# A two-block transformer step in one kernel: the first mixer's query rows made once, their turned halves moved by transfers

## The reference, cut to what matters

```python
c_q, c_kv, k_rope = split(h @ w_in)            # 384, 256 and 32 columns
q  = (rmsnorm(c_q, q_norm) @ w_uq).reshape(B, S, 16, 64 + 32)
kv = (rmsnorm(c_kv, kv_norm) @ w_ukv).reshape(B, S, 16, 64 + 64)
q_rope = apply_rotary(q[..., 64:], cos, sin)   # x1*cos - x2*sin, x1*sin + x2*cos
k_rope = apply_rotary(k_rope, cos, sin)        # one for all 16 heads
s = (q_nope @ k_nope^T + q_rope @ k_rope^T) * scale
o = softmax(causal(s)) @ v
```

## Time and profile before

| | us |
|---|---|
| median of 3 runs | 1406.35 |
| lowest, highest | 1406.14, 1406.98 |
| the profiled execution | 1407.12 |
| its span in the profile | 1405.3 |
| TensorE busy | 1392.9 |
| VectorE, ScalarE, GpSimd busy | 915.3, 740.8, 73.9 |

### The profile page before, as it was taken

One profiled execution on the slowest core, in us unless ns is written; L12 is line 12 of the kernel. 1 busy time (PEld: TensorE's weight loads), 2 busy tenths in 40 slices (PEclk: granted clock), 3 DMA queues, 4 the chain that ended last, 5 costly groups with the idle time before them and its releaser, 6 DMA issues.

```text
span 1405.3 us, 21648 instructions
## 1 busy us (share of the span) xinstructions
PE 1392.9 (99%) x8384; PEld 1237.7 (88%) x8384; DVE 915.3 (65%) x1170; ACT 740.8 (53%) x913; POOL 73.9 (5%) x113
## 2 busy tenths in 40 slices
PE   9999999999999999999999999999999999999997
PEld 8989989988888888899888888888889999888886
DVE  5555787675566666677666666756567676665656
ACT  6656673344355444557554444544445558554444
POOL 2000010010020000010120000000000002200000
PEclk9999999999999999999999999999999999999999
DMA  8534441255535555462375554655545410555552
GB/s 312 205 141 149 153 149 61 91 195 195 193 133 204 201 184 191 168 206 80 126 268 197 193 201 174 244 188 203 181 179 184 156 51 2 204 200 183 198 185 90
DMA packets 34767, 239.60 MB, mean 170 GB/s; under 512 B 3914, under 2 KB 4058, under 8 KB 6928
## 3 DMA queue, kind: packets, MB, share of 16 engines
q1 hardware_dynamic: 32832, 231.39, 46.2%
q0 software_dynamic: 1440, 6.67, 1.4%
q10 hardware_dynamic: 432, 0.66, 0.1%
HBM read 237.10 MB, written 1.08 MB: 169 GB/s over the span
## 4 chain that ended last, share of the span: by engine, by line
PE 95%; ACT 2%; DVE 2%; issue 1%; POOL 0%; POOLq 0%; ACTq 0%; DVEq 0%
PE ps L737 22%; PE ps L707 15%; PE ps L709 15%; PE ps L708 15%; PE ps L745 11%; PE ps L1038 3%; PE ps L1012 2%; PE ps L1022 1%; PE ps L1360 1%; PE ps L2949 1%; PE ps L2957 1%; PE ps L646 1%; PE ps L2961 1%; PE ps L3127 1%; PE ps L828 1%
## 5 line engine op out<-in xcount | busy, mean ns | idle before, releaser
L413 DVE TENSOR_TENSOR low<-raw,high 128x2048 fp32r<-128x2048 f32 (+1 forms) x212 | 481.3, 2272 | 231.3 <-ACT high L407 228.7
L407 ACT ACTIVATE high<-raw 128x2048 fp32r<-128x2048 f32 (+1 forms) x215 | 406.5, 1893 | 75.7 <-PE ps L709 71.4
L737 PE MATMUL ps<-nt,high 128*128 128x512 f32 x1344 | 320.1, 390 | 0.0
L737 PEld LDWEIGHTS ps<-nt,high 128*128 128x128 f32 x1344 | 249.0, 188 | 49.8
L745 PEld LDWEIGHTS ps<-nt,low 128*128 128x128 f32 x1344 | 167.5, 189 | 3.6
L745 PE MATMUL ps<-nt,low 128*128 128x256 f32 x1344 | 168.6, 283 | 0.0
L707 PE MATMUL ps<-high,hth 128*128 128x512 f32 x320 | 124.5, 389 | 0.0
L708 PE MATMUL ps<-low,hth 128*128 128x512 f32 x320 | 124.5, 389 | 0.0
L709 PE MATMUL ps<-high,htl 128*128 128x512 f32 x320 | 124.5, 389 | 0.0
L707 PE MATMUL ps<-nt,high 128*128 128x256 f32 x400 | 114.3, 286 | 0.0
L709 PE MATMUL ps<-nt,low 128*128 128x256 f32 x400 | 113.3, 283 | 0.0
(11 more groups left out here) (425 smaller groups left out, 2076.0 us busy)
## 6 DMA issues: line engine op xcount, KB each, us to landing
raw<-in_stream SPq DMA_DIRECT2D x215, 1024.0 KB, 4.8
late<-in_w POOLq DMA_DIRECT2D x1, 2048.0 KB, 9.4
scr<-bias_by_distance POOLq DMA_DIRECT2D x1, 2048.0 KB, 14.9
scr<-in_mem SPq DMA_DIRECT2D x2, 512.0 KB, 5.0
raw<-in_stream SPq DMA_DIRECT2D x4, 256.0 KB, 6.6
raw<-in_stream SPq DMA_DIRECT2D x2, 512.0 KB, 7.7
x<-in_x SPq DMA_DIRECT2D x1, 1024.0 KB, 8.5
con<-in_con SPq DMA_DIRECT2D x1, 592.0 KB, 8.9
```

The costliest lines, as they stand in the source:

```text
L407: nc.scalar.activation(high_of(t, slice(0, n)), raw[t % SLOTS][:, 0:n], ACT.Copy).then_inc(w_high, 1)
L413: nc.vector.tensor_tensor(low_of(t, slice(0, n)), raw[t % SLOTS][:, 0:n], high_of(t, slice(0, n)).bitcast(F32), ALU.subtract).then_inc(w_l ...
L737: last = nc.tensor.matmul(r3(bank, 2), w[:, k, P * j:P * j + P], nt[:, :, k, :], start=first and k == 0, stop=not first and k == KC - 1, s ...
```

## The change

- `uq` becomes three tiles. uq0 holds the rotary rows of all 16 heads, 512 columns; uq1 and uq2 the plain rows, 64 for each head, eight heads a tile. The exchanged rotary rows are gone, and so is the tile `uq3`; the stream has 216 tiles.
- For uq0, VectorE multiplies each bank of 128 rows by a cosine table and by a sine table (with signs) into `ml_turned[0]` and `ml_turned[1]`, with no wait between the two (L2598 of the kernel after). SyncE's queue then moves them with eight transfers (32 partitions x 4 heads x 256) to rows 64 to 95 and 96 to 127 of `mq`. They stand behind tile `uv` in its program, and wait for both banks (`ml_qd` 2).
- The key's rotary part is made as 32 rotated rows and 32 rows with the halves exchanged, in 64 partitions, so that the dot product over 128 rows adds the cosine products times the one and the sine products times the other. GpSimd's queue copies all 64 rows under each head. The scores contract over 128 rows in place of 96.
- The plain rows of uq1 and uq2 hold two heads per 128 rows: ScalarE copies partitions 0 to 63 and VectorE partitions 64 to 127 of each bank.
- The spread of the roots, its copy and the products with it move from behind uq1 to behind its first bank. `ml_kvhigh` and `ml_kvlow` stay at uq2's place, which is now directly before `uk`.
- The loop of SyncE's stream is cut in two around tiles uv, mlao0 and mlao1; constants change by 64 KB.

```diff
-    t += ["mlain0", "mlain1", "mlain2"] + [f"uq{j}" for j in range(4)] + ["uk", "uv"]
+    t += ["mlain0", "mlain1", "mlain2"] + [f"uq{j}" for j in range(3)] + ["uk", "uv"]
...
+            def sp_turned_queries(sp):
+                sp.wait_ge(ml_qd, 2)
+                for j in range(4):
+                    for n in range(2):
+                        sp.dma_start(mq[64 + 32 * n:96 + 32 * n, j::4, :], ml_turned[n][32 * j:32 * j + 32])\
+                            .then_inc(ml_qrd, 16)
+
+            latent = TILE["uv"] // SLOTS
+            sp_tiles(sp, 2, latent)
+            for t in range(SLOTS * latent, SLOTS * latent + SLOTS):
+                sp_tile(sp, t)
+                if t == TILE["uv"]:
+                    sp_turned_queries(sp)
...
-            pool.dma_start(mk_[64:96, :, :], rep(mlc["kr"][64:96, S:2 * S], MLA_H)).then_inc(ml_krd, 16)
+            pool.dma_start(mk_[64:128, :, :], rep(mlc["kr"][64:128, S:2 * S], MLA_H)).then_inc(ml_krd, 16)
...
-            for j in range(4):
+            act_step(act, "uq0")
+            for j in (1, 2):
                 act_step(act, f"uq{j}")
                 if j == 2:
                     act.wait_ge(ml_kvm, 1)
                     nc.scalar.activation(ch_[:, 3:5, :], m_kvn, ACT.Copy).then_inc(ml_kvhigh, 1)
...
-                if j == 1:
-                    act.wait_ge(ml_spread, 1)
-                    nc.scalar.activation(m_rows, ps[7][:, :], ACT.Copy).then_inc(ml_rows, 1)
+                    if j == 1 and b == 0:
+                        act.wait_ge(ml_spread, 1)
+                        nc.scalar.activation(m_rows, ps[7][:, :], ACT.Copy).then_inc(ml_rows, 1)
...
-                    if j + b:
-                        dve.wait_ge(ml_qd, 2 * j + b)
-                    h = 4 * j + 2 * b
-                    rotate(ps[2 * (j % 2) + b], 2, mq[64:96, h:h + 2, :]).then_inc(ml_qd, 1)
+                    bank = ps[2 * (j % 2) + b]
+                    if j:
+                        h = 8 * (j - 1) + 4 * b
+                        nc.vector.tensor_copy(mq[0:64, h + 1:h + 4:2, :], r3(bank[64:128, :], 2)).then_inc(ml_qd, 1)
+                    else:
+                        for n, table in enumerate((cos_, sin_)):
+                            last = nc.vector.tensor_tensor(ml_turned[n][:, 2 * b:2 * b + 2, :], r3(bank, 2), rep(table, 2),
+                                                           ALU.mult)
+                        last.then_inc(ml_qd, 1)
...
-                if j == 1:
-                    pe.wait_ge(ml_diag, 4)
-                    for n in range(4):
-                        last = nc.tensor.matmul(pair(ps[7], n), ones, m_diag[:, n, :], start=True, stop=True)
-                    last.then_inc(ml_spread, 1)
+                    if j == 1 and b == 0:
+                        pe.wait_ge(ml_diag, 4)
+                        for n in range(4):
+                            last = nc.tensor.matmul(pair(ps[7], n), ones, m_diag[:, n, :], start=True, stop=True)
+                        last.then_inc(ml_spread, 1)
...
+            pe.wait_ge(ml_qrd, 16 * 8)
```

More of the change, by code:

```diff
@@ L84 @@
 GATE_AND_UP = {f"f{f}{part}{i}" for f in range(4) for part in "gu" for i in range(FT)}
-USED = {"ba": KC * P, "ng": KC * P, "uq0": 1536, "uq1": 1536, "uq2": 1536, "uq3": 1536}
+USED = {"ba": KC * P, "ng": KC * P, "uq0": 1536, "uq1": 1536, "uq2": 1536}
 TILE = {n: i for i, n in enumerate(PLAN)}
@@ L128, in constants @@
     put("upto", (j <= i) * 1.0)
-    put("before", (j < i) * 1.0)
     put("ones", np.ones((P, P)))
@@ L223, in lay_out @@
     q = wuq.reshape(MLA_QL, MLA_H, MLA_N + MLA_R)
-    q = np.concatenate([q, q[:, :, 80:96], q[:, :, 64:80]], axis=2).reshape(MLA_QL, MLA_H * P)
-    for j in range(4):
-        put(f"uq{j}", cols(q, 512 * j, 512))
+    nope, rope = (np.ascontiguousarray(v).reshape(MLA_QL, -1) for v in (q[:, :, :MLA_N], q[:, :, MLA_N:]))
+    put("uq0", cols(rope, 0, 512))
+    for j in range(2):
+        put(f"uq{j + 1}", cols(nope, 512 * j, 512))
     kv = wukv.reshape(MLA_KVL, MLA_H, 2, 64)
@@ L358, in build @@
         mlc = carve(late, [("rot", 512), ("kr", 512)], 1280)
+        ml_turned = [r3(ml["y"][:, 1024 * n:1024 * n + 1024], 4) for n in range(2)]
         mls = carve(late, [("kv", 512), ("kvn", 512), ("diag", 512), ("v0", 1040)], 4352)
@@ L1824, in _, with sp_tiles, sp_tile @@
                     sp.dma_start(row[:], A["row"]).then_inc(row_here, 16)
[L1825 to L1833 removed]
+            def sp_tiles(sp, first, end):
+                with sp.Fori(first, end) as i:
+                    for c in range(SLOTS):
+                        tile = sp.snap(i * SLOTS + c)
+                        sp.wait_ge(w_low, i * SLOTS + (c - SLOTS + 1))
+                        sp.dma_start(raw[c][:], A["stream"][bass.ds(tile, 1)].rearrange("o p w -> (o p) w"))\
+                            .then_inc(raw_here[c], 16)
+            def sp_tile(sp, t):
+                sp.wait_ge(w_low, t - SLOTS + 1)
+                sp.dma_start(raw[t % SLOTS][:], A["stream"][t]).then_inc(raw_here[t % SLOTS], 16)
+            def sp_turned_queries(sp):
[10 more added lines that the diff above has]
+                    sp_turned_queries(sp)
+            sp_tiles(sp, latent + 1, NT // SLOTS)
+            for t in range(NT // SLOTS * SLOTS, NT):
+                sp_tile(sp, t)
             for t in range(TT):
@@ L3043, in _ @@
             C_ = (ch_, cl_)
-            for j in range(4):
+            for j in range(3):
                 t = TILE[f"uq{j}"]
```

79 lines of the change are left out of this document (35 added, 44 removed).

## The result

The changed kernel takes 1409.26 us (median of 8 runs, 1407.49 to 1412.93) beside 1406.47 us for the kernel before on the same chip: ratio 1.0025, interval 1.0015 to 1.0034 (ratio and interval go by all the runs; the two medians alone give 1.0020). It is slower by 2.8 us, where 1405.9 with a range up to 1407.8 was forecast. The profiled execution took 1408.44 us, span 1406.6.

What follows compares the result with a forecast made beforehand. TensorE's stream was taken to bound the kernel; -4.3 us for the tile, +2.5 and +1.4 us for two waits gave -0.4 us, so 1405.9 us after setting the profiled sum to the median, range 1402.05 to 1407.8.

Steps and rivals of the forecast that it cites:

- the bound: TensorE's stream sets the kernel's time; work of VectorE, ScalarE or a queue counts only where TensorE waits for it.
- step 1: Three uq tiles instead of four take 36 matmuls out of TensorE's stream: -4.3 us.
- step 2: At the roots' spread, half a tile sooner, TensorE waits for GpSimd's diagonals beside uk's split: +2.5 us.
- step 3: Before uk, TensorE waits for VectorE's low parts of the keys' latent: +1.4 us.
- Edits that I cost at nothing: Key's rotation and copy, eight transfers, 128-row scores and larger constants: each held at 0, within 0.6 us.
- the issue time: On SyncE's queue behind uv, eight transfers issue at 0.33 us each, so mlao0 goes out near 622.9 us.
- Rival D: Eight transfers hold SyncE's queue, mlao0 lands late and the scores wait: +9.1 us, 1415.45 us; chance 0.15.
- C: Rival: neither the wait before the spread nor that before uk binds, full -4.3 us, 1402.05 us; chance 0.15.

Runs made afterwards that it cites:

- e10: Changed kernel with the eight transfers behind mlao0, the latent's parts ahead of uv's splits and uk's low split behind the root products: 1402.19 us, ratio 0.9967.
- e6: Changed kernel with the eight transfers behind mlao1 and VectorE's split of uk behind the products with the roots: 1413.84 us, ratio 1.0053.
- e5: Changed kernel with the eight transfers behind mlao1 and the latent's high and low parts ahead of uv's splits: 1405.99 us, ratio 0.9995.
- e3: Changed kernel with the eight transfers behind mlao1 instead of uv in SyncE's program: 1405.59 us, ratio 0.9993.
- e12: Changed kernel with only the eight transfers moved behind mlao0 in SyncE's program: 1405.77 us, ratio 0.9996.
- e1: Changed kernel with the eight transfers of the turned queries left out, for times only: 1405.52 us, ratio 0.9993.
- e7: Changed kernel with the eight transfers behind mlao1 and the edits of e5 and e6 together: 1413.75 us, ratio 1.0057.
- e4: Changed kernel with the roots' spread, its copy and its products back behind uq1's second bank: 1411.19 us, ratio 1.0032.
- e11: Changed kernel with the latent's parts ahead of uv's splits and uk's low split behind the root products, SyncE's order untouched: 1409.8 us, ratio 1.0024.
- e2: Changed kernel with the key's copy cut to 32 partitions, the other 32 rows zeroed earlier, for times only: 1405.63 us, ratio 0.9990.
- e8: Changed kernel with latent's parts ahead of uv's splits, uk's low split behind root products, key's root spread early and its copy at 616.8 us: 1405.21 us, ratio 0.9995.
- e9: e8 with the eight transfers behind mlao0 instead of uv in SyncE's program: 1401.95 us, ratio 0.9968.

## Why the prediction was wrong, point by point

**Right: the bound, and step 1.** TensorE's stream sets the time, and a `uq` tile is worth 4.3 us of it: e10, in which no wait is left, has a profiled execution of 1402.72 us, 4.4 under that of before.

**Right: step 2**, 2.5 us forecast from start to start, 2.31 measured in the same way (2.15 as idle time). The diagonals ended 0.60 us behind uk's split (0.52 in the row it was taken from), and without the split beside them took 0.72 us (e6). The Trainium skill, "SBUF — State Buffer", section "SBUF: two separate sides", has the port pair taken by whichever starts first; here VectorE's record starts 0.09 us ahead of GpSimd's and GpSimd pays, so the trace agrees.

**Right: step 3**, 1.4 forecast, 1.58 from start to start (1.43 as idle time), by the chain as it was written (bank copy, split, split, low parts); e5 takes it away by ordering alone. The two steps miss by 0.2 us each in opposite directions, and so the sum came out closer than its terms: in e3 and e12, where only the third wait is gone, the scores start 0.44 us sooner behind uq0's sums than before, against the -0.4 of the forecast.

**Wrong: "Edits that I cost at nothing", the key's copy.** It was given 5.4 to 10.8 us, "which is hidden", with 640.8 us (14.9) as the far end; it took 16.7. The step read its duration from a transfer in whose 5.4 us the engines still had time free (busy for 0.77 of it, from 626.5 to 631.9 us), and doubled it for its size. By size alone that was near enough (9.0 in e1). What the step left out is that the change itself fills those engines: it puts 1 MB of transfers in front of two tiles of 1 MB and so moves them into the same stretch as the copy. The numbers for that were in the working, mlao0 near 622.9 and the copy near 625.9, but what that stretch asks of the engines was never added up. The missed term is +2.84 us: it turns -0.4 into +2.4.

**Wrong: the issue time.** Eight at 0.33 us each were taken from the tiles; they took 5.25 us, 0.59 to 0.72 each, and up to 10.44 (e7) when tiles and the copy were landing beside them. That held the tiles back from a forecast 622.9 to 624.59, though this execution ran 0.7 us early.

**Not foreseen: the clock.** The forecast priced waits by their length alone. At waits of about 5 us and more the granted clock fell to 1.2 GHz in every profile that has one (e4, e6, e7, e11), and behind one of 2.15 us in one (e2); three of the changed kernel's eight runs carry a lower mean clock. The median is 2.8 us up, where the profiled execution is 1.3 us up. The clock is not what broke the forecast: the five runs without a lower mean have a median of 1408.58 us, which is outside the range as well.

**Rival D** named the right queue and the wrong victim: mlao0 was in time in the changed kernel, and became what ended last in e8 and e11. The argument against D misread: 0.33 us is how long one issue lasts, not how far apart the tiles go out (four of them between 616 and 635 us), so that row shows no overlap of transfers. The eight do overlap: issued 0.6 to 0.7 us apart, each landed after 2.3 to 2.5 us. **C** would have needed both waits to be absent, and they were not; its time is what e9 and e10 reach.

Another cause for the slow copy has to be weighed. The Trainium skill, "SBUF — State Buffer", section "SBUF: two separate sides", says in its box on transfers issued from GpSimd's queue that VectorE, while it runs an operation in a two-port mode, keeps GpSimd from writing their descriptors, and that the DMA engines then sit idle. This case speaks against it. The engines were not idle: 0.93 busy from 625.4 to 642.1 us. In e1 VectorE has the same instructions at the same distance from the copy as in the changed kernel (the split 2.5 us behind its issue), and it took 9.0 us. In e11 two splits overlap the copy, from 623.26 and from 626.67 us, and it took 10.0.

What stays open: by what rule the engines divide their time once both queues have work under way (59 to 40% in the changed kernel). The runs show that a transfer issued about a microsecond or two behind one of the other queue hardly moves until that one is through.

## What to carry to other kernels

A transfer that is "hidden" has to be priced in the traffic of its own stretch after the change, so add up what all queues there ask of the DMA engines, the transfers that the change holds back included. Add it up in engine time and not in bytes: 1 MB of the key's copy costs them 2.7 times what 1 MB of a tile does. When an instruction is moved on one engine, follow what it frees as well: a split of VectorE frees a slot, the slot lets a tile out, and everything behind that tile on SyncE's queue moves with it. And with several waits in a row, taking away the first ones shows nothing until the last is gone: e11 looks like no gain, and with one more line the same edits are worth 0.3%.

## What the runs showed of the hardware

- A copy of 1 MB within the chip's SBUF, one 64-partition source to 16 places: 9.0 us without the eight transfers (e1), 9.2 to 12.4 where at most one tile had gone out in the 4 us ahead of it, 16.7 and 17.0 with two tiles issued just ahead of it (the changed kernel and e4).
- The engines' time: busy for 0.97 with 151 GB/s while only this copy runs, for 0.85 with 356 GB/s while only a tile does (e1).
- Two queues: a tile issued 1.3 us behind the copy took 13.1 us (e11), one issued 2.3 us behind it 11.8 (e10); a tile issued 0.8 us ahead of it took 5.5, and the copy 16.7 (the changed kernel).
- Eight transfers of 128 KB from SBUF to SBUF: 5.25 us of SyncE's time to issue, and 7.85 to 10.44 us when the engines are full.
- Two small diagonals on GpSimd, together: 0.72 us, or 2.79 beside one split of VectorE from two SBUF operands.
- TensorE's granted clock stayed full behind waits of 1.4 to 2.7 us in all profiles but e2's, where it fell behind one of 2.15 us (0.53 from 624 to 626 us). It fell to 0.50 in waits of 4.95, 5.7, 8.3 and 9.4 us, before TensorE had gone on, and was full again 3 to 6 us after.
